# A decoder layer on one core: another order of the expert work, and other engines for its activation

## The reference, cut to what matters

```python
def clamped_swiglu(gu):
    gate = jnp.minimum(gu[..., :D_FF], SWIGLU_LIMIT)                    # 7.0
    up = jnp.clip(gu[..., D_FF:], -SWIGLU_LIMIT, SWIGLU_LIMIT)
    return gate * jax.nn.sigmoid(SWIGLU_ALPHA * gate) * (up + 1.0)      # 1.702

def expert_block(args):                    # one block of up to 128 tokens of expert e
    xb, e = args
    gu = xb @ w_gate_up[e] + b_gate_up[e]                 # 1024 -> 2048
    return clamped_swiglu(gu) @ w_down[e] + b_down[e]     # 1024 -> 1024
```

## Time and profile before

| | |
|---|---|
| time of the profiled execution | 2052.51 us |
| its span, first to last instruction | 2050.7 us |
| median of the runs | 2052.74 us |
| PE busy | 1735.6 us, 85% |
| DVE busy | 1387.2 us, 68% |
| ACT busy | 1139.0 us, 56% |
| POOL busy | 750.7 us, 37% |
| mean granted clock of TensorE | 0.929 |
| moved by DMA | 495.48 MB |

### The profile page before, as it was taken

One profiled execution on the slowest core, in us unless ns is written; L12 is line 12 of the kernel. 1 busy time (PEld: TensorE's weight loads), 2 busy tenths in 40 slices (PEclk: granted clock), 3 DMA queues, 4 the chain that ended last, 5 costly groups with the idle time before them and its releaser, 6 DMA issues.

```text
span 2050.7 us, 27433 instructions
## 1 busy us (share of the span) xinstructions
PE 1735.6 (85%) x7534; PEld 1318.5 (64%) x7535; DVE 1387.2 (68%) x1345; ACT 1139.0 (56%) x1162; POOL 750.7 (37%) x438
## 2 busy tenths in 40 slices
PE   6999966782799898899999889898999989888880
PEld 1788844441677676777777677676777767667660
DVE  0444469453778887458788888854688888655865
ACT  2322244411677776456777777753677777635750
POOL 2000000113345454334545554533444554433541
PEclk9999976985899999999999999999999999999995
DMA  7666330023799999559999999974799999846956
GB/s 224 224 231 205 103 116 0 27 77 117 245 330 322 310 311 304 184 186 309 306 319 320 312 308 325 331 265 135 235 325 319 304 316 325 298 138 206 316 191 245
DMA packets 380688, 495.48 MB, mean 242 GB/s; under 512 B 21051, under 2 KB 284311, under 8 KB 380049
## 3 DMA queue, kind: packets, MB, share of 16 engines
q1 hardware_dynamic: 363456, 458.27, 66.8%
q0 software_dynamic: 14592, 34.72, 4.9%
q10 hardware_dynamic: 2610, 2.11, 0.3%
HBM read 490.75 MB, written 27.09 MB: 253 GB/s over the span
## 4 chain that ended last, share of the span: by engine, by line
PE 51%; issue 13%; DVE 9%; DMA 3%; POOL 2%; ACT 2%; POOLq 0%; DVEq 0%; SPq 0%; ACTq 0%
PE ps L1011 14%; PE ps L1013 14%; PE ps L1012 14%; DVE wl L1126 3%; PE ps L622 3%; PE ps L960 2%; PE ps L1007 2%; DVE gsu L1161 2%; POOL gsu L1249 1%; DVE gsu L1157 1%; PE ps L972 1%; DMA rawm<-in_w_gate_up 1%; DMA yt<-expert_rows 1%; ACT wh L1040 1%; DVE gsu L1156 1%
## 5 line engine op out<-in xcount | busy, mean ns | idle before, releaser
L1126 DVE TENSOR_TENSOR wl<-rawm,wh 128x2048 fp32r<-128x2048 f32 x320 | 781.4, 2458 | 129.8 <-ACT wh L1040 129.2
L1040 ACT ACTIVATE wh<-rawm 128x2048 fp32r<-128x2048 f32 x384 | 730.5, 1912 | 176.0 <-PE ps L1013 108.1
L1011 PE MATMUL ps<-wh,xh 128*128 128x512 f32 x1120 | 471.3, 421 | 25.1 <-POOL wl L1254 25.1
L1013 PE MATMUL ps<-wh,xl 128*128 128x512 f32 x1120 | 440.2, 393 | 0.0
L1012 PE MATMUL ps<-wl,xh 128*128 128x512 f32 x1120 | 439.8, 393 | 0.0
L1249 POOL TENSOR_TENSOR gsu<-gsu 128x256 f32<-128x256 f32 x140 | 206.3, 1474 | 433.4 <-DVE gsu L1161 386.4
L1254 POOL TENSOR_TENSOR wl<-rawm,wh 128x2048 fp32r<-128x2048 f32 x64 | 339.4, 5303 | 19.2 <-ACT wh L1040 19.1
L1011 PEld LDWEIGHTS ps<-wh,xh 128*128 128x128 f32 x1120 | 213.9, 191 | 75.9 <-issue 36.5
L1011 PE MATMUL ps<-wh,ah 128*128 128x512 f32 x560 | 247.1, 441 | 0.0
L1013 PEld LDWEIGHTS ps<-wh,xl 128*128 128x128 f32 x1120 | 212.1, 189 | 46.7
L1012 PEld LDWEIGHTS ps<-wl,xh 128*128 128x128 f32 x1120 | 212.9, 190 | 42.7
(11 more groups left out here) (233 smaller groups left out, 2042.7 us busy)
## 6 DMA issues: line engine op xcount, KB each, us to landing
rawm<-in_w_gate_up SPq DMA_DIRECT2D x512, 512.0 KB, 4.9
rawm<-in_w_down SPq DMA_DIRECT2D x128, 1024.0 KB, 5.6
raw<-in_w_ada SPq DMA_DIRECT2D x24, 1024.0 KB, 5.3
raw<-in_w_in SPq DMA_DIRECT2D x16, 1024.0 KB, 5.2
yt<-expert_rows POOLq DMA_DIRECT2D x4, 2048.0 KB, 9.2
wo<-in_w_out SPq DMA_DIRECT2D x2, 2048.0 KB, 17.5
bias_vectors_repeated<-bias_vectors POOLq DMA_DIRECT2D x1, 2304.0 KB, 16.4
xs<-in_x ACTq DMA_DIRECT2D x1, 2048.0 KB, 25.6
```

The source lines that it names most:

```text
L1011: nc.tensor.matmul(dst, a_h[:, b, kk, :], wh[:, v % SPL, k, :], start=False, stop=False)
L1013: ins = nc.tensor.matmul(dst, a_l[:, b, kk, :], wh[:, v % SPL, k, :], start=False, stop=kk == KC - 1)
L1040: nc.scalar.activation(flat(wh[:, v % SPL, :, :]), flat(rawm[:, v % RAW, :, :]), ACT.Copy).then_inc(wh_done, 1)
L1126: nc.vector.tensor_tensor(flat(wl[:, v % SPL, :, :]), flat(rawm[:, v % RAW, :, :]), flat(wh[:, v % SPL, :, :]), ALU.subtract).then_inc(wl_ ...
```

## The change

- Order: the loop's iteration e now does gate and up of e (8 halves), the token transposes of e + 1, down of e - 1 (4 halves), and then all transposes of the activation of e. Down of the last expert stands behind the loop. The loop's body holds two experts (`passes`), with the first and the last expert outside it.
- Tiles: gate and up are no longer side by side. For each of two tiles of 512 columns there are two halves of gate (into bank 0) and two of up (into bank 1); a further block uses its one bank for gate and up in turn. Each half is one DMA.
- Activation: ACT takes the sigmoid of the gate straight out of PSUM, not clamped, into `actv` (`gate`). DVE multiplies it by the gate out of PSUM (`gate_product`); this frees the gate's bank. DVE clamps up between 1 - 7 and 1 + 7 (`up`; the 1 is added to the bias once, ahead), which frees up's bank, and the last product takes the minimum with 7 sigmoid(1.702 x 7) and multiplies. POOL has only the indirect DMAs and their index copies left.
- Buffers: 8 places of weights in which `rawm` and `wl` are the same memory, so a place is free once PE has used the half; `wh` stays at 4. Tokens and outputs of a block share `xy[b]`, so the gather of e + 1 waits for the scatter of e - 1.
- DVE has all 12 `split_low`.

```diff
-RAW, SPL = 4, 4
-POOL_LOW = (7, 11)
-DVE_LOW = tuple(v for v in range(HALVES) if v not in POOL_LOW)
+RAW, SPL = 8, 4
+GATE_MAX = LIMIT / (1.0 + math.exp(-ALPHA * LIMIT))
...
-    wh = at("wh", [P, SPL, HK, UN], F32R, 32 * KB)
-    wl = at("wl", [P, SPL, HK, UN], F32R, 64 * KB)
+    wl = at("wl", [P, RAW, HK, UN], F32R, 0)
+    wh = at("wh", [P, SPL, HK, UN], F32R, 64 * KB)
...
+    def passes(eng, body):
+
+        body(0, Place(0, 0), False)
+        with eng.Fori(0, E // 2 - 1) as k:
+            body(2 * k + 1, Place(3 * k + 1, 0), True)
+            body(2 * k + 2, Place(3 * k + 2, 4), True)
+        k = E // 2 - 1
+        body(E - 1, Place(3 * k + 1, 0), True)
...
# SP
+        def load(place, v, src, free=True):
+            if free:
+                sp.wait_ge(half_used, place.count(v) - RAW)
+            sp.dma_start(rawm[:, place.slot(v), :, :], src).then_inc(rawm_in[place.slot(v)], 16)
...
# PE, ahead of the first matmul of an even gate or up half
                     if b == 0:
+                        if t == 0 and before is not None:
+                            pe.wait_ge(y_half_copied[up], before.earlier(1, 0))
+                        elif t:
+                            pe.wait_ge((u_ready if up else g_ready)[0], x.count(T_GU, 0, 0))
+                    elif up:
+                        pe.wait_ge(g_ready[1], x.count(T_GU, t, b))
+                    elif t:
+                        pe.wait_ge(u_ready[1], x.count(T_GU, 0, b))
...
# PE, ahead of an even down half, block 0
+                        pe.wait_ge((u_ready if t else g_ready)[0], (x.e + (1 if after is None else 2)) * T_GU + START)
...
# PE
+        def body(e, place, has_d):
+            x = Expert(pe, e)
+            before = Expert(pe, e - 1) if has_d else None
+            for v in range(N_GU):
+                gate_up_half_used(x, before, place, v)
+            last = is_last(e)
+            if not last:
+                tokens_transposed(Expert(pe, e + 1), e + 1)
+            if has_d:
+                for d in range(N_D):
+                    down_half_used(before, x, place, N_GU + d, d)
+            act_transposed(x, last)
...
# ACT
+        def split_high(place, v, first=False):
+            act.wait_ge(rawm_in[place.slot(v)], place.arrivals(v))
+            if not first:
+                act.wait_ge(half_used, place.count(v) - SPL)
...
+            if has_d:
+                act_high(before, before.further)
+            for v in range(N_GU + N_D if has_d else N_GU):
+                split_high(place, v + SPL)
+                if v == 0 and has_d:
+                    act_high(before, at_once)
+                if v in (1, 5):
+                    gate(x, v // 4, place, v)
+                if v == 7 and not is_last(e):
+                    after = Expert(act, e + 1)
+                    tokens_high(after)
+                if v in (9, 11):
+                    outputs(before, v // 2 - 4, place, v, after)
...
# DVE
+            if has_d:
+                act_low(before, before.further)
+            for v in range(N_GU + N_D if has_d else N_GU):
+                if v in (3, 7):
+                    up(x, v // 4, place, v)
+                if v == 8 and not is_last(e):
+                    tokens_low(Expert(dve, e + 1))
+                if v in (2, 6):
+                    gate_product(x, v // 4, x.further)
+                split_low(place, v + SPL)
+                if v in (2, 6):
+                    gate_product(x, v // 4, at_once)
+                if v == 0 and has_d:
+                    act_low(before, at_once)
...
# POOL
+        def body(e, gathers=True):
+            if not (isinstance(e, int) and e < 2):
+                scatter(Expert(pool, e - 2))
+            if gathers:
+                gather(Expert(pool, e + 1), None if isinstance(e, int) and e == 0 else Expert(pool, e - 1))
```

More of the change, by code:

```diff
@@ L898, in further, with __init__, slot, loaded_before @@
                         work(b)
[L900 to L920, removed]
+    class Place:
+        def __init__(self, q, r):
+            self.q, self.r = q, r
+        def slot(self, v):
+            return (self.r + v) % RAW
+        def loaded_before(self, v):
+            return (11, 11, 10, 10, 0, 0, 0, 0)[self.slot(v)]
+        def split(self, v):
+            return (self.r + v) % SPL
+        def arrivals(self, v):
+            return 16 * (self.q + (self.r + v) // RAW + 1 + self.loaded_before(v))
+        def count(self, v):
+            return RAW * self.q + self.r + v + 1
+    def passes(eng, body):
[5 more added lines that the diff above has]
+        body(E - 1, Place(3 * k + 1, 0), True)
+    def is_last(e):
+        return isinstance(e, int) and e == E - 1
+    LAST = Place(3 * (E // 2 - 1) + 2, 4)
+    def gate_up_half(e, v):
+        t, up, h = v // 4, v // 2 % 2, v % 2
+        return w_gate_up[0, bass.ds(e, 1), h * HK * P:(h + 1) * HK * P, up * FF + UN * t:up * FF + UN * (t + 1)].rearrange(
+            "a (k p) n -> p (a k) n", p=P)
+    def down_half(e, d):
+        t, h = d // 2, d % 2
+        return w_down[0, bass.ds(e, 1), h * HK * P:(h + 1) * HK * P, UN * t:UN * (t + 1)].rearrange(
+            "a (k p) n -> p (a k) n", p=P)
     def experts_sync(sp):
@@ L926, in experts_sync, with tokens_transposed @@
             sp.wait_ge(h2_out[w], 32)
[L928 to L943, removed]
+        def load(place, v, src, free=True):
[4 more added lines that the diff above has]
+            for v in range(N_GU):
+                if not has_d and v == 6:
+                    sp.wait_ge(lg_ps, TC)
+                load(place, v, gate_up_half(e, v), free=has_d)
+            if has_d:
+                for d in range(N_D):
+                    load(place, N_GU + d, down_half(e - 1, d))
+        passes(sp, body)
+        for d in range(N_D):
+            load(LAST, d, down_half(E - 1, d))
     def experts_pe(pe):
         pe.wait_ge(nk_ready, 1)
-        def tokens_transposed(x):
+        def tokens_transposed(x, e):
+            if not (isinstance(e, int) and e == 0):
+                pe.wait_ge(al_done[0], e - 1 + START)
             def work(b):
@@ L974, in work, with multiply @@
                 ins.then_inc(at_done[m], 1)
             x.blocks(work)
-        def half(x, v):
-            u, h = v // 2, v % 2
-            wait_low(pe, x.e, v)
+        def multiply(dst, place, v, b, h, a_h, a_l):
+            for k in range(HK):
+                kk = HK * h + k
+                nc.tensor.matmul(dst, a_h[:, b, kk, :], wh[:, place.split(v), k, :], start=False, stop=False)
+                nc.tensor.matmul(dst, a_h[:, b, kk, :], wl[:, place.slot(v), k, :], start=False, stop=False)
+                ins = nc.tensor.matmul(dst, a_l[:, b, kk, :], wh[:, place.split(v), k, :], start=False, stop=kk == KC - 1)
+            return ins
@@ L1003, in work @@
[L1003 to L1013, removed]
+                        if t == 0 and before is not None:
[6 more added lines that the diff above has]
+                        pe.wait_ge(u_ready[1], x.count(T_GU, 0, b))
+                    elif before is not None:
+                        pe.wait_ge(y_copied[1], before.earlier(U_D, 1))
@@ L1033, in experts_act @@
+        passes(pe, body)
+        end = Expert(pe, E - 1)
+        for d in range(N_D):
+            down_half_used(end, None, LAST, d, d)
     def experts_act(act):
         act.wait_ge(nk_ready, 1)
[L1036 to L1040, removed]
+        act.wait_ge(lg_ps, TC)
@@ L1115, in experts_act @@
[L1115 to L1127 removed]
+            before = Expert(act, e - 1) if has_d else None
@@ new lines, in experts_act, with split_low @@
+        passes(act, body)
+        end = Expert(act, E - 1)
+        act_high(end, end.blocks)
+        outputs(end, 0, LAST, 1, None)
+        outputs(end, 1, LAST, 3, None)
+    def experts_dve(dve):
+        def split_low(place, v):
+            dve.wait_ge(wh_done, place.count(v))
+            nc.vector.tensor_tensor(flat(wl[:, place.slot(v), :, :]), flat(rawm[:, place.slot(v), :, :]),
+                                    flat(wh[:, place.split(v), :, :]), ALU.subtract).then_inc(wl_done, 1)
@@ L1143, in act_low, with gate_product @@
             blocks(work)
-        def gate_up(x, t):
+        def gate_product(x, t, blocks):
             def work(b):
-                m, s = min(b, 1), (1 + b if b else t % 2)
-                bank = 1 + b if b else t % 2
+                m = min(b, 1)
+                dve.wait_ge(s_done[m], x.count(T_GU, t, b))
+                dst = actv[:, b, UN * t:UN * (t + 1)]
+                nc.vector.tensor_tensor(dst, dst, ps[:, 1 + b if b else 0, :], ALU.mult).then_inc(g_ready[m], 1)
+            blocks(work)
@@ L1150, in work, with up @@
+        def up(x, t, place, v):
+            def work(b):
+                m = min(b, 1)
+                dst = actv[:, b, UN * t:UN * (t + 1)]
                 if b:
[L1151 to L1156 removed]
@@ L1169, in experts_dve, with body @@
         tokens_low(Expert(dve, 0))
-        with dve.Fori(0, E) as e:
```

(34 more changed lines are left out.)

270 lines of the change are left out of this document (116 added, 154 removed).

## The result

| | before | after |
|---|---|---|
| median of the runs | 2052.72 us | 2163.76 us (2154.82 to 2167.04) |
| span of the profiled execution | 2050.7 us | 2165.3 us |
| mean granted clock of TensorE | 0.929 | 0.908 |
| PE, DVE, ACT, POOL busy | 1735.6, 1387.2, 1139.0, 750.7 us | 1749.4, 1361.1, 1026.2, 218.9 us |

The changed kernel is slower: ratio 1.053, 95% interval 1.0489 to 1.0571, 111 us. The forecast was 2131, range 2042 to 2168. PE does the same work in a longer span, and DVE, ACT and POOL are all busy for less time.

What follows compares the result with a forecast made beforehand. PE was taken to bound the kernel, with its own waits on POOL and the loads right beside it. 2052.5 + 53 (31 periods) + 25 (two-block experts) + 1 (start and end) = 2131 us, +3.8%, range 2042 to 2168.

Steps and rivals of the forecast that it cites:

- The chain at the gate's bank: Half 4 waits for DVE's gate product behind half 6's split: 5.2 us chain, 2.6 late; the same chain at half 8.
- the table loads: ACT, two-expert loop body: both loads of 1.28 us fall on the first expert, so its half 4 starts 5.0 us late.
- The alternation: PE's wait at half 4: 2.6 us in one expert and 5 in the next, from the table loads.
- the same work costs no gap: Register work at the loop's end, ahead of 1027.75, costs PE no gap, so 1.2 us of issue an expert goes.
- The clock: PE returns at 1.2 GHz behind long waits: 0 to 1.7 us lost for each of two, 1.2 taken an expert.
- Experts with two blocks: Waits at the further block's single bank and at transposes: 58 us extra instead of 49.5, +8 each, +25 for three.
- POOL: PE's waits for POOL's product and `wl` go, with issue and half-clock time: about 4.5 to 5 us an expert.
- Rival A: Waits on POOL were all there was; half 4 does not wait: 37.4 us an expert, 1940 to 1988 us; chance 0.14.
- Loads: Weight loads cost nothing: 12.6 MB in a 42.8 us period, each load issued 4 halves ahead of its split.
- rival C: The gather comes late behind the scatter on one buffer: 31 x 3 and more, 2220 us; chance 0.07.
- Start: Ahead of the experts' loop: eight places of weights are loaded at once, -4 us.
- End: Down of the last expert has nothing to hide its split, +5 us.

Runs made afterwards that it cites:

- e2: Changed kernel with DVE's gate product of block 0 ahead of the split of half 6 (and 10) instead of behind it; 2053.96 us, ratio 1.0011.
- e1: Changed kernel with the code for a third and fourth block of an expert left out on every engine; 2100.96 us, ratio 1.0246.
- e4: Kernel before with only PE's loop written for two experts in each iteration, same instructions in the same order; 2175.6 us, ratio 1.0624.
- e8: Changed kernel with a one-expert loop body and 6 places of weights, all four blocks' code, gate product still behind the split; 2109.23 us, ratio 1.0292.
- e3: Changed kernel with the edits of e1 and e2 together; 1966.38 us, ratio 0.9583.
- e7: e3 with a second PSUM bank for an expert's second block, gate and up in turn; 1918.79 us, ratio 0.9361.
- e6: Kernel before without wide arithmetic on POOL: DVE makes all 12 splits and the activation's last product; 2014.53 us, ratio 0.9827.

## Why the prediction was right, and where it was not

*Direction and size*: forecast +78, measured +111, inside the range. The chain at the gate's bank, the main reason given, is shown. But the size is in part luck: one term of the sum (the table loads) measured nothing, and a loss about as large that the sum did not have (the jump back) stood in its place.

The sum against the two profiled executions (2050.7 and 2165.3 us) comes apart as follows. In the new order five halves, 14 us, are done behind the last expert's token split that were done ahead of it before; they are put back in the periods here.

| us | forecast | measured |
|---|---|---|
| ahead of the first token split | -4 | +4 |
| 31 ordinary periods | +53 (41.1 to 42.8) | +63 (41.2 to 43.2) |
| three second blocks | +25 (49.5 to 58 each) | +33 (mean 51.4 to 62.5) |
| end | +5 | +14 |

*The gate's bank.* Shown by e2. These are ACT's split of half 6, which starts as PE ends half 2, and the product that frees the bank:

```profile
1157.90 1.92 ACT L1100 ACTIVATE wh<-rawm 128x2048 fp32r<-128x2048 f32 x1 [0.58 <-PE ps L1011]
...
1162.07 0.68 DVE L1202 TENSOR_TENSOR actv<-actv,ps 128x512 f32<-128x512 f32 x1
```

From 1157.90 to half 4's start at 1162.80 it took 4.9 us, forecast 5.2; PE's idle time ahead of half 4 was 2.22, forecast 2.6. At half 8 from 1171.66 to 1176.64, 5.0, forecast 5.2. It was read from the order of the code and three durations; e2 removes it by one moved instruction. An expert without the jump and without clock loss takes 39.9 us, forecast 40.4.

*Table loads.* Wrong. The step was "both loads fall on the first of each two". The changed kernel has one table load in all its expert code, in the first expert, and none in the loop:

```profile
L1117 ACT ACT_TABLE_LOAD x1 | 1.3, 1283 | 0.0
```

The kernel before had one ahead of a split in each iteration, and 34 ahead of a sigmoid; there the loop was entered without a sigmoid before it, here the first expert stands outside and has one. That this is the reason was not tried. The term was 1.2 us an expert in the mean, 37 us; without it the same sum gives 2094, still in the range.

*The alternation.* An alternation came, but not the one forecast. Forecast were 2.4 us from one expert to the next, as a wait at half 4 of 2.6 and 5.0 in turn. The wait at half 4 is 2.22 in every ordinary expert of the loop, and the periods differ by 5.5 to 6.0 from something else: the jump back. The prediction said of the work at the loop's end that "the same work costs no gap", from the row ahead of 1027.75. True of a body of one expert; the body was doubled, and the row could not speak for that. The sum priced nothing for the jump, which costs 4.36 idle and 1.5 of clock in the expert shown and 63 us in all, and e1, e4 and e8 show what it is.

*The clock.* Forecast 1.2 an expert, bounds 0 and 1.7 for a wait. Periods of one kind come in two lengths, 39.9 and 41.5, or 45.4 and 47.2: with and without about 1.6 us. A wait of 2.22 us was not followed by a loss each time: behind the one at 1289.72 the granted clock is 0.50 from 1291.7 to 1293.7, behind the one at 1162.80 two halves take the 5.7 us of full clock. In e3, without waits, it is never there. In the mean, 43.2 less 39.9 is 3.3 us: 1.8 of idle time at the jump and 1.5 of clock, a part of it behind the jump (estimate from these means).

*Experts with two blocks.* Forecast 58 us for one more block. Measured from 768.46 to 1005.22, 236.8 us for four periods; less four at the mean of 43.2 this leaves 64 (64 and 59 in the other two). The forecast had the waits right: 5.2 and 5.2 for the single bank, 2.8 at half 10, 6 and 5.8 at the transposes; the trace has 4.93, 4.93, 2.49, 5.99 and 4.59. e7 shows that 16 us are the single bank's three waits; forecast for these were 13 and some clock. Why the rest is larger than forecast was not tried. Before, the extra was 49.5 in the expert that the prediction read, 52.6 and 52.1 in the other two.

*POOL.* That its part pays is shown by e6, 37 us; the forecast had 4.5 to 5 us an expert for it with the issue gap, and e3's 35.9 against 41.1 shows 5.2 for the whole of the old gaps. Rival A, that only these gaps counted, is close to what e3 is: its forecast for that case, 37.4 an expert, is near the 35.9 measured. It fell for this kernel, since the new chain was real.

*Loads.* Forecast nothing, and right: ACT waits for none. *The gather* (rival C) did not come late: after the first expert PE never waits for it. That rival's price was also summed wrong, since 8 us late in 31 periods are 248 us and not 93. *Start*: forecast -4, and it came out at +4: the first tokens are split at 518.8 us instead of 514.4. POOL waits 4.78 us for the small transfers that make the tables instead of 2.77, behind eight loads of 1 MB; that is 2 of the 4 us, and the rest is open (with the same eight loads it is 518.4 to 524.2 in e1, e2, e3 and e7). *End*: forecast +5, measured +14; three waits of 2.28, 2.37 and 4.65 us stand there, and the other 5 us are open.

*What adds up.* Changed kernel +111. Without the chain and the jump it would be -86 (e3). Taking out the chain alone gives 110, the jump alone 63, and 24 go only when both are gone.

## What to carry to other kernels

When a change makes one engine free a PSUM bank behind other work of its own, walk the whole ring: which instruction stands ahead of the release, what it waits for, and whether that waits for the matmul engine itself. One such ring of 5 us against 2.7 us of cover, at halves 4 and 8, cost 110 us here, more than all that the rest of the change won, and one moved instruction removed it. And the length of a loop's body is a cost of its own: before unrolling, or before code for rare cases goes into a loop, look at the instruction queue's packets and at the wait behind the jump back.

## What the hardware showed that was not expected

- A loop's body of more than some length makes PE wait at the jump back: 3.1 to 4.5 us in the changed kernel, 3.0 to 4.7 in e2, 2.7 to 8.0 in e4. The instruction queue moves 214 and 232 packets instead of 16 to 27. Code under an `If` that is never taken counts (e1). No run shows the fetch itself; that PE waits for instructions is inferred from the packets, from the wait put down to issue and from what the length of the body does in e1, e4 and e8. The limit lies between bodies with 576 and with 1152 matmuls of the halves and was not narrowed down, and why e4's waits are longer stays open. e4 shows it for PE's code alone; whether ACT's and DVE's doubled code adds to it in the changed kernel was not tried.
- With weights in pieces of 2 KB for each partition (512 columns) in place of 1 KB, DMA moves more at about the same busy share: 360 GB/s at 1.01 in e3, against 331 GB/s in the best slice of the kernel before and 329 at 0.98 in e6, which has its tiles (560 to 760 us). e3's period of 35.9 would not have fitted the old rate: its 12.9 MB at 331 GB/s are 39 us (estimate from the two rates and e3's period). So the wider tiles, which showed nothing in the changed kernel, probably carry the fast versions; no run has the new order with the old tiles.
- DVE's instructions run at one length once POOL does no wide arithmetic. In the changed kernel all 384 splits take 2.278 to 2.296 us, where the mean was 2.46. e6 takes only POOL's arithmetic out of the kernel before: there the longest split falls from 3.105 to 2.356 us, and the longest product of up and gate (L1161) from 4.647 to 0.428 us, with 0.424 the shortest in both.
